# Adding up squares on VectorE ahead of one matmul with ones, in a hybrid decoder trunk

## What is computed

```python
def rmsnorm(x, g):
    x32 = x.astype(jnp.float32)
    y = x32 * lax.rsqrt(jnp.mean(x32 * x32, axis=-1, keepdims=True) + EPS)
    return (y * g.astype(jnp.float32)).astype(x.dtype)
```

## Time and profile before

| | before |
|---|---|
| median of 3 runs | 2585.38 us (2585.14 to 2587.1) |
| the profiled execution | 2584.86 us, span 2583.2 us |
| TensorE busy | 2417.3 us, 94% |
| VectorE busy | 1481.9 us, 57% |
| ScalarE busy | 784.4 us, 30% |
| granted clock, mean | 0.975 of full |

### The profile page before, as it was taken

The page is one execution under the profiler, slowest core; times in us unless marked ns, Lnnn a source line. Parts: engine busy times, 40 slices in busy tenths (PEclk is TensorE's granted clock), DMA queues, the critical chain, the costliest instruction groups (busy, mean ns, idle before and its releaser), DMA issues.

```text
span 2583.2 us, 26796 instructions
## 1 busy us (share of the span) xinstructions
PE 2417.3 (94%) x10851; PEld 1928.3 (75%) x10851; DVE 1481.9 (57%) x2204; ACT 784.4 (30%) x1204; POOL 61.7 (2%) x51
## 2 busy tenths in 40 slices
PE   7995899999999999998898888689999999999997
PEld 5883678888777888876676676577688888888885
DVE  6998499896544444437777677665433332333333
ACT  5211332223433222234444444432321121121113
POOL 0000000000000000021100110000000000000000
PEclk9997999999999999999999999899999999999998
DMA  3110223333323333320110010211111111111111
GB/s 127 42 49 17 66 82 97 91 92 95 91 82 89 91 95 101 97 59 29 33 33 28 26 33 17 86 30 48 41 43 47 50 45 53 49 45 53 49 33 66
DMA packets 279192, 155.13 MB, mean 60 GB/s; under 512 B 5701, under 2 KB 273310, under 8 KB 279070
## 3 DMA queue, kind: packets, MB, share of 16 engines
q1 hardware_dynamic: 279070, 153.42, 19.9%
HBM read 145.54 MB, written 7.86 MB: 59 GB/s over the span
## 4 chain that ended last, share of the span: by engine, by line
PE 80%; DVE 15%; ACT 2%; issue 2%; DMA 1%; SPq 0%; DVEq 0%; ACTq 0%
PE ps L1363 25%; PE ps L1365 25%; PE ps L1364 25%; PE ps L1422 3%; DVE cacc L973 2%; DVE cvA L973 2%; PE ps L1346 2%; DVE rb L1210 1%; DVE sc L1189 1%; DVE Wl L1135 1%; ACT sc L771 1%; DVE sc L1187 1%; DVE Wl L901 1%; DVE ATl L1203 1%; PE ps L1593 1%
## 5 line engine op out<-in xcount | busy, mean ns | idle before, releaser
L1363 PE MATMUL ps<-Sh,Wl 128*128 128x512 f32 x2304 | 943.1, 409 | 25.7 <-DVE Sl L1005 9.9
L1364 PE MATMUL ps<-Sl,Wh 128*128 128x512 f32 x2304 | 906.9, 394 | 0.0
L1365 PE MATMUL ps<-Sh,Wh 128*128 128x512 f32 x2304 | 906.8, 394 | 0.0
L1363 PEld LDWEIGHTS ps<-Sh,Wl 128*128 128x128 f32 x2304 | 438.6, 190 | 142.0 <-issue 42.6
L1364 PEld LDWEIGHTS ps<-Sl,Wh 128*128 128x128 f32 x2304 | 438.9, 191 | 94.0 <-issue 10.6
L1365 PEld LDWEIGHTS ps<-Sh,Wh 128*128 128x128 f32 x2304 | 438.0, 190 | 94.2
L901 DVE TENSOR_TENSOR Wl<-raw,Wh 128x1024 fp32r<-128x1024 f32 (+3 forms) x246 | 285.5, 1161 | 132.0 <-ACT Wh L593 130.7
L593 ACT ACTIVATE Wh<-raw 128x1024 fp32r<-128x1024 f32 (+3 forms) x246 | 245.8, 1003 | 321.4 <-PE ps L1365 164.9
L1085 DVE TENSOR_TENSOR xT<-ps,xT 128x512 f32<-128x512 f32 x112 | 77.2, 689 | 241.9 <-PE ps L1365 241.9
L1078 DVE TENSOR_TENSOR tmp<-ps,rstd 128x512 f32<-128x512 f32 x66 | 45.6, 691 | 167.3 <-PE ps L1365 167.3
L1363 PE MATMUL ps<-G0h,Wl 128*128 128x512 f32 x352 | 138.6, 394 | 0.0
(11 more groups left out here) (159 smaller groups left out, 2664.8 us busy)
## 6 DMA issues: line engine op xcount, KB each, us to landing
raw<-in_ffn_w_dram SPq DMA_DIRECT2D x148, 512.0 KB, 3.8
raw<-in_pw_w_dram SPq DMA_DIRECT2D x32, 512.0 KB, 3.7
raw<-in_ffn_w_dram SPq DMA_DIRECT2D x32, 448.0 KB, 3.5
raw<-in_ffn_w_dram SPq DMA_DIRECT2D x24, 384.0 KB, 3.2
xrow<-in_x_dram SPq DMA_DIRECT2D x8, 512.0 KB, 7.5
raw<-in_w_q_dram SPq DMA_DIRECT2D x8, 512.0 KB, 3.9
raw<-in_w_k_dram SPq DMA_DIRECT2D x8, 512.0 KB, 3.7
raw<-in_w_v_dram SPq DMA_DIRECT2D x8, 512.0 KB, 4.2
```

What stands on the lines that cost most here:

```text
L1363: pe.matmul(dst, ll, rh, start=start, stop=False)
L1364: pe.matmul(dst, lh, rl, start=False, stop=False)
L1365: return pe.matmul(dst, lh, rh, start=False, stop=stop)
```

## The change

For SUM_F0A, SUM_F0B, SUM_ATT_A, SUM_ATT_B and both halves of SUM_F1, six sums, ScalarE writes the first square straight to an accumulator (`mu` in SBUF, or `acc1` for F1's two halves). VectorE adds the seven others to it (`add_square` on VectorE), and one matmul with ones then sums over partitions (`sum_up`). The two LayerNorm sums and the two at the end stay as they are. In F1 the high and low part of the third weight block are made ahead of the squares and adds, where they stood at the FFN's first block.

```diff
@@ -120,8 +120,23 @@
+ADDED_UP = (SUM_F0A, SUM_F0B, SUM_ATT_A, SUM_ATT_B, SUM_F1)
+SUM_MATMULS = (KC, 1, KC, 1, 1, 1, 2, 2 * KC)
 def square(v, k, hf=0):
     return v * KC + k if v < SUM_F1 else (SUM_F1 + 2 * (v - SUM_F1)) * KC + 2 * k + hf
+def sums_through(v, j):
+    return sum(SUM_MATMULS[:v]) + j + 1
+def squares_added(v, k, hf=0):
+    return ADDED_UP.index(v) * (KC - 1) + (k if v < SUM_F1 else 2 * k - 1 + hf)
...
@@ -258,6 +273,7 @@
         sq1 = at("sq1", [P, 2, HT], F32, R_AT + 4 * KB)
+        acc1 = at("acc1", [P, 2, HT], F32, R_AT)
         ATh = at("ATh", [P, TB, 2 * P], F32R, G_AT)
...
@@ -563,16 +580,27 @@
         def _(act):
-            def squares(i, buf, src, ready, value):
+            def squares(v, n, src, ready, value, hf=0):
                 act.wait_ge(ready, value)
-                if i >= 2:
-                    act.wait_ge(sum_mm, i - 1)
-                act.activation(buf[:, i % 2, :] if len(src.shape) == 2 else by_block(buf[:, i % 2, :]), src,
-                               ACT.Square).then_inc(sq_ok, 1)
-            def root(n, hf, i, bank=5):
-                act.wait_ge(sum_mm, i + 1)
+                j = n if v < SUM_F1 else 2 * n + hf
+                buf = sq if v < SUM_F1 else sq1
+                if v in ADDED_UP:
+                    dst = buf[:, (j - 1) % 2 if v < SUM_F1 else j % 2, :]
+                    if n == 0:
+                        dst = mu[:, :] if v < SUM_F1 else acc1[:, hf, :]
+                    elif n >= 3:
+                        act.wait_ge(acc_ok, squares_added(v, n - 2) if v < SUM_F1 else squares_added(v, n - 1, hf))
+                    elif n == 2 and v == SUM_F1:
+                        act.wait_ge(acc_ok, squares_added(v, 1, hf))
+                else:
+                    dst = buf[:, j % 2, :]
+                    if j >= 2:
+                        act.wait_ge(sum_mm, sums_through(v, j - 2))
+                act.activation(dst if len(src.shape) == 2 else by_block(dst), src, ACT.Square).then_inc(sq_ok, 1)
+            def root(n, hf, v, j=0, bank=5):
+                act.wait_ge(sum_mm, sums_through(v, j))
                 act.activation(rstd[:, hf, :], ps[:, bank, :], ACT.Sqrt, bias=eps, scale=1.0 / D).then_inc(std_ok, 1)
...
@@ -873,17 +901,18 @@
                                    scale=col("ffn_norm_g", KC + n)).then_inc(s_hi, 1)
+            hi(F1.block0 + 2)
             for n in range(KC):
                 for hf in F1.halves:
-                    squares(square(SUM_F1, n, hf), sq1, X(n, hf), wo_ev, 4 * KC)
+                    squares(SUM_F1, n, X(n, hf), wo_ev, 4 * KC, hf)
             for hf in F1.halves:
-                root(6 + hf, hf, square(SUM_F1, KC - 1, hf), 6 + hf)
+                root(6 + hf, hf, SUM_F1, hf, 6 + hf)
             ffn(F1, lambda i: None)
...
                 for hf in F1.halves:
-                    squares(square(SUM_END, n, hf), sq1, X(n, hf), add_ok, F1.last_added(n, hf) + 1)
+                    squares(SUM_END, n, X(n, hf), add_ok, F1.last_added(n, hf) + 1, hf)
             for hf in F1.halves:
-                root(8 + hf, hf, square(SUM_END, KC - 1, hf), 6 + hf)
+                root(8 + hf, hf, SUM_END, 2 * KC - 2 + hf, 6 + hf)
             for t in range(TB):
...
@@ -900,6 +929,14 @@
                                   flat(Wh[s][:, 0:n, :]).bitcast(F32), ALU.subtract).then_inc(w_lo, 1)
+            def add_square(v, n, hf=0):
+                to, buf, j = (mu[:, :], sq, n - 1) if v < SUM_F1 else (acc1[:, hf, :], sq1, hf)
+                dve.wait_ge(sq_ok, square(v, n, hf) + 1)
+                if n > 1:
+                    dve.wait_ge(acc_ok, squares_added(v, n - 1, hf))
+                dve.tensor_tensor(to, to, buf[:, j % 2, :], ALU.add).then_inc(acc_ok, 1)
...
@@ -1025,6 +1062,9 @@
                 pw2_out(LA, n)
+                if n >= 2:
+                    add_square(SUM_F0A, n - 1)
+            add_square(SUM_F0A, KC - 1)
             recip(1, LA)
...
@@ -1056,7 +1096,8 @@
                         left = None
-                    lo(b + 2)
+                    if f is not F1 or i:
+                        lo(b + 2)
                     beside(i)
...
@@ -1115,6 +1156,9 @@
                     operand_low(OP_F0B * KC + n - 1, LB, n - 1, col("ffn_norm_g", n - 1))
+                if n >= 2:
+                    add_square(SUM_F0B, n - 1)
+            add_square(SUM_F0B, KC - 1)
             operand_low(OP_F0B * KC + KC - 1, LB, KC - 1, col("ffn_norm_g", KC - 1))
...
@@ -1122,12 +1166,16 @@
                     operand_low(OP_ATT * KC + i - ATT_SPLIT_AT, LA, i - ATT_SPLIT_AT)
+                    if i > ATT_SPLIT_AT:
+                        add_square(SUM_ATT_A, i - ATT_SPLIT_AT)
                 if i == ATT_ROOT_AT:
...
                 operand_low((OP_ATT + 1) * KC + n, LB, n)
+            for n in range(1, KC):
+                add_square(SUM_ATT_B, n)
...
@@ -1328,6 +1376,10 @@
                     operand_low(OP_F1 * KC + 2 * n + hf, hf, n, col("ffn_norm_g", KC + n))
+            lo(F1.block0 + 2)
+            for n in range(1, KC):
+                for hf in F1.halves:
+                    add_square(SUM_F1, n, hf)
             for hf in F1.halves:
...
@@ -1415,12 +1467,17 @@
                     pe.wait_ge(xr_ev, 2 * KC)
-                elif n == 0 and v < SUM_F1:
-                    pe.wait_ge(std_ok, v)
                 elif n == 0:
-                    pe.wait_ge(std_ok, 6 if v == SUM_F1 else 8)
+                    pe.wait_ge(std_ok, v if v < SUM_F1 else 8)
                 pe.matmul(ps[:, bank, :], ones[:, :], (sq if v < SUM_F1 else sq1)[:, i % 2, :], start=n == 0,
                           stop=n == KC - 1).then_inc(sum_mm, 1)
+            def sum_up(v, hf=0, bank=5):
+                pe.wait_ge(acc_ok, squares_added(v, KC - 1, hf))
+                pe.wait_ge(std_ok, v)
+                pe.matmul(ps[:, bank, :], ones[:, :], mu[:, :] if v < SUM_F1 else acc1[:, hf, :], start=True,
+                          stop=True).then_inc(sum_mm, 1)
...
@@ -1448,9 +1505,7 @@
                 dense(PW2A + n, n % 4, Sh[:, LA], Sl[:, LA], KC, free, value, s_ready(OP_LN_A * KC) if n == 0 else None)
-                if n:
-                    add_square(SUM_F0A, n - 1)
-            add_square(SUM_F0A, KC - 1)
+            sum_up(SUM_F0A)
...
@@ -1496,13 +1551,11 @@
                 dense(PW2B + n, n % 4, Sh[:, LA], Sl[:, LA], KC, free, value, s_ready(OP_LN_B * KC) if n == 0 else None)
-                if n:
-                    add_square(SUM_F0B, n - 1)
-            add_square(SUM_F0B, KC - 1)
+            sum_up(SUM_F0B)
             def beside_f0b(i):
-                if ATT_SPLIT_AT < i <= ATT_SPLIT_AT + KC:
-                    add_square(SUM_ATT_A, i - ATT_SPLIT_AT - 1)
+                if i == ATT_SPLIT_AT + KC:
+                    sum_up(SUM_ATT_A)
...
@@ -1660,9 +1713,8 @@
             for turn, m in enumerate(FIRST_ORDER):
-                if turn in (1, 2):
-                    for n in range(4 * (turn - 1), 4 * turn):
-                        add_square(SUM_ATT_B, n)
+                if turn == 2:
+                    sum_up(SUM_ATT_B)
                 project(0, m, 0, KC, turn)
...
@@ -1682,9 +1734,8 @@
                 if i == 0:
-                    for n in range(KC):
-                        for hf in F1.halves:
-                            add_square(SUM_F1, n, hf, 6 + hf)
+                    for hf in F1.halves:
+                        sum_up(SUM_F1, hf, 6 + hf)
```

More of the change, by code:

```diff
@@ L331, in trunk @@
         sq_ok = sem("sq_ok")
+        acc_ok = sem("acc_ok")
         sum_mm = sem("sum_mm")
@@ L639, in ln_square @@
             def ln_square(hf, n):
-                squares(square(SUM_LN_B if hf else SUM_LN_A, n), sq, (cvB if hf else cvA)[:, n, :],
-                        xc_ok, KC * hf + n + 1)
+                squares(SUM_LN_B if hf else SUM_LN_A, n, (cvB if hf else cvA)[:, n, :], xc_ok, KC * hf + n + 1)
             def ln_split(hf, n):
@@ L654, in _ @@
                 ln_square(LA, n)
-            root(0, LA, square(SUM_LN_A, KC - 1))
+            root(0, LA, SUM_LN_A, KC - 1)
             for n in range(KC):
@@ L660, in _ @@
                 hi(PW2A + n + 2)
-                squares(square(SUM_F0A, n), sq, X(n, LA), x_ok, n + 1)
-            root(1, LA, square(SUM_F0A, KC - 1))
+                squares(SUM_F0A, n, X(n, LA), x_ok, n + 1)
+            root(1, LA, SUM_F0A)
             for n in range(KC):
@@ L668, in ffn @@
                 for i, (g, what, c, b) in enumerate(f.order()):
-                    hi(b + 2)
+                    if f is not F1 or i:
+                        hi(b + 2)
                     beside(i)
@@ L696, in beside_f0a @@
                 if i == ROOT_AT:
-                    root(2, LB, square(SUM_LN_B, KC - 1))
+                    root(2, LB, SUM_LN_B, KC - 1)
                 if SPLIT_AT <= i < SPLIT_AT + 4:
@@ L707, in _ @@
                                scale=col("ffn_norm_g", n)).then_inc(s_hi, 1)
```

(10 more changed lines are left out.)

## The result

The changed kernel takes 2560.36 us in the median (2558.12 to 2564.98, 4 runs), beside 2585.84 us for the kernel before; the ratio is 0.9903, 95% interval 0.9891 to 0.9914. That is 25.5 us less. Forecast were 28.8 us less and a range of 2551.0 to 2564.5. The profiled execution has a span of 2558.1 us, 25.1 less than before.

A forecast was written before the change was run, and what follows sets the result against it. TensorE, busy for 94% of the span, was taken as the bound. The terms -4.7 - 4.7 - 6.3 - 6.0 - 8.8 + 1.7 = -28.8 us gave 2556.6 us in the median, range 2551 to 2564.5.

The forecast's parts named there:

- What one square costs: TensorE, matmuls with ones: each removed square is worth 0.91 us; the net 42 would be 38 us.
- First half's F0 sum: End of the first half's second projection: six squares save 5.4 us, the longer end costs 0.7, in all -4.7 us.
- Second half's F0 sum: Before the second half's first FFN: six squares save 5.4 us, a later sum costs 0.7, in all -4.7 us.
- none for the 2.6 us before the second FFN: TensorE's 2.6 us stall before the second FFN: no clock fall in the sum, one left to the range.
- Attention's sum, first half: Beside the second half's FFN: seven adds hide under products, seven squares of 0.91 us go, -6.3 us.
- Attention's sum, second half: After attention's second projection: sum done at 1135.4 instead of 1141.4, with TensorE waiting 0.3 us, -6.0 us.
- the 0.72 us between dependent adds: Attention's second-half sum: dependent adds on VectorE start 0.72 us apart, so the last ends at 1134.4.
- F1's sums: Start of F1: turns of 1.38 us, TensorE waits 4 us, -8.8 us; one clock fall costs +1.7.
- The page's rule on idle gaps: No TensorE gaps over about 3 us: F1's stall costs a fall, the 2.6 us one none, sum -28.8.
- The reading by the row at 1154.39: A 1.92 us stall was followed by half speed, so both new stalls cost a fall: sum -27.1.
- The first: Rival: sums wait longer, add and square at 0.95 us, clock falls at both stalls: 2563.6 us, chance 0.16.
- The other three: Rivals: small stalls, 2552.7, chance 0.12; weight-bound blocks beside squares, 2573.7, 0.02; slow F1 add chain, 2588.9, 0.01.

The follow-up runs named there:

- the run with one sum alone: Kernel before, with only SUM_ATT_A (beside the second half's FFN) added up on VectorE: 2579.58 us, ratio 0.9975.
- the last run: Changed kernel with F1's sums after the second block, SUM_F0B's after the first, SUM_LN_B and both SUM_END added up on VectorE: 2530.65 us, ratio 0.9789.

## Why the prediction was right, and where it was off

The direction, the mechanism and the range held; the gain is 3.3 us short of the 28.8 forecast. Half of that is one fall of the clock that the sum left out and the range took in.

- **What one square costs.** 0.91 us held to within 0.1 us for seven of them in the run with one sum alone.
- **First half's F0 sum.** Forecast -4.7, measured -4.5; the end is 0.7 us longer, as counted. This stage took 56.4 to 56.9 us in the profiles that have this sum, so the 0.2 is of the size of that spread.
- **Second half's F0 sum.** Forecast -4.7, measured -3.05 (9.40 less the 6.35 of the single run). The step that failed is "none for the 2.6 us before the second FFN": the clock fell. The sum started 4.68 us earlier, as counted, so the fall makes all of the miss, 1.6 us. The stall was 2.90 us for 2.6. Moving the sum gave back stall and fall, 4.8 us.
- **Attention's sum, first half.** Forecast -6.3, measured -6.35. The adds are hidden; three times as many moved the stage by 0.4 us, in one wait of TensorE.
- **Attention's sum, second half.** Forecast -6.0, measured -5.5. The term that was mis-sized is the 0.72 us between dependent adds. It was read off two other instructions, 0.03 us apart; behind an add 0.10 us pass before the next, which makes 0.795, and six of these make the missing 0.4. The squares were ready.
- **F1's sums.** Forecast -8.8 + 1.7 = -7.1, measured -6.0. Two terms were mis-sized. The adds started when counted, but turns took 1.45 us for 1.38, so the sum came 0.4 us later (6 x 0.07); it is the same 0.10 us behind an add, here before ScalarE's next square. And the fall costs 2.7 us and not 1.7: it was counted with 3.4 us at half speed and had 6.8, of which the stall hid the first 1.3. Together -8.8 + 0.4 + 2.7 = -5.7, and from F1's start to its last product the two traces differ by just that. The other 0.3 stands behind it, in the 16 squares at the end, which nothing has changed: from F1's last product to the transposes it is 25.4 us before and 25.1 in every other profile that has these squares, so they are no gain of the change.
- **The page's rule on idle gaps.** In the prediction, the Trainium skill's "TensorE: Matmul & The Clock Gate" (section "Why this matters for your kernels") would have cleared the stall before the second FFN. The trace speaks against it. In all seven profiles that have the stall before this sum, of 2.90 to 2.99 us, the clock fell. A stall of 3.09 to 3.11 us in attention passed without a fall in eight of the eleven profiles and met one in three; one of 1.91 or 1.92 us ahead of attention's fourth projection met a fall in eight and not in three. So a length alone doesn't decide in this range, and a fall has to be allowed for behind stalls of this size. The reading by the row at 1154.39, both fall, gave -27.1 and was nearer.
- **The rivals.** The first (add and square at 0.95 us, both falls) had the falls right and the turns wrong; it gave 2563.6. The measured 2560.4 lies 3.2 us below that and 3.8 above the forecast's own 2556.6, so the number alone speaks for neither; it is the turn of 1.45 us for two adds that decides. The other three did not come.

The falls in attention, left to the range, moved this stage by up to 3 us between executions (646.1 to 649.2 us in ten profiles, 643.7 in the last run). The -0.4 us of the changed kernel aren't among them: it has 61 us at half speed there, as before, and what they come from is open.

## What to carry to other kernels

Where a matmul with ones only adds chunks up before it sums over partitions, the adding belongs on an engine with room, and each removed matmul is worth its full time where TensorE is the bound: 0.91 us here. Look for such sums everywhere, the end included (12 us here, which the change had left out). Then see that the last add doesn't become a wait: take the sum one block later if the result isn't wanted at once. Count a stall of TensorE of about 3 us or more at its own length and put the clock's fall into the range: it cost 1.6 us behind the stall of 2.90 here and 2.7 behind that of 4.68. Read such effects by stage rather than in the total.

## What the runs showed of the hardware

- A hand-over isn't the same both ways. In F1's chain an add on VectorE starts 0.03 us after ScalarE's square ends, and ScalarE's next square 0.10 us after the add. Between two dependent adds on VectorE 0.10 us pass as well (0.795 us from start to start). The 0.15 to 0.22 us that the rows show as idle time before these are counted from the engine's own last instruction, not from what released it.
- A fall of the clock costs by the time that TensorE then works at half. In F1 PEclk was 0.50 for 6.8 us in the changed kernel, where it fell 1.3 us before TensorE went on, and the cost was 2.7 us. It was the same in four other profiles with this stall, with falls 1.0 to 1.2 us before. In the run with two buffers per half it fell 0.3 us after TensorE went on and stayed for 3.4 us, which fits the 1 us less that the fall cost. Matmuls with no use, put into the stall, kept PEclk at 1.00.
- Independent 128x512 adds in SBUF start 0.60 us apart on VectorE (14 in 8.51 us), although each is shown with 0.68.
